# V as the stationary operand in two column groups, a joining product, split scores for two attentions, and the sink as a score column, in a fused four-layer attention kernel

## The chip, the cores and the metric

The kernel runs on one core of one Trainium2 chip. The metric is the device time of one execution in microseconds; a row of the profile is one core's.

## What is computed

Two blocks of two layers each follow one another on 512 rows of width 1024, with a context of 256 rows in the first block. Layer 1 has two attentions side by side, mla (8 heads, 96 wide, V 64 wide) and gqa (8 heads, 2 key heads, 64 wide), over 768 keys (512 rows and 256 of context). Layer 2 has win: 8 heads, 64 wide, a window of three blocks of 128 keys plus the context, and a sink logit per head that takes part in the softmax but has no V. Cut to its core:

```python
def joint_dense_attention(q, k, v, kc, vc):          # gqa and mla
    kk, vv = concat([kc, k]), concat([vc, v])
    sc = einsum('bqkgd,bnkd->bkgqn', qi, kk) * d ** -0.5
    p = softmax(sc)
    return einsum('bkgqn,bnkd->bqkgd', p, vv)

def joint_window_attention(q, k, v, kc, vc, sink):   # win
    s_loc = where(mask, einsum(qi, ki) * scale, NEG_INF)
    s_ctx = einsum(qi, kc) * scale
    p = softmax(concat([s_ctx, s_loc, s_snk]))
    return einsum(p[:l], vc) + einsum(p[l:l + 3 * Q_BLOCK], vi)
```

Layers 3 and 4 (attentions diff, fox and odd, V 128 wide) have the same structure and are not touched. All of it is float32.

## The kernel before

The work is written out by hand, engine by engine, with semaphores. `to(name, key)` increments one, `at(name, key)` waits for it. Each engine's program is strictly in the order written. TensorE's order sets that of everything else: projections in1 and up, attention gqa, attention mla, projections out1 and in2, attention win, out2, in3, attentions diff and fox, and so on.

Projections split both operands into a high and a low part in fp32r and add three products (L839 to L841). A plain fp32 matmul appears in the trace as two weight loads and two MATMUL instructions; one of split parts (fp32r) and a transpose (L1020, L954) as one each.

An attention is a list of units, one for a head and a tile t of 128 query rows. In gqa and mla a head has the units t = 0, 4, 1, 5, 2, 3: tiles 0 to 3 see all six blocks of 128 keys, tiles 4 and 5 (the context) two. In win a head has tiles 0 to 3 with 4, 5, 5 and 4 blocks. Iteration j of the loop works on three units at once:

- TensorE: the scores of unit j into banks 0 and 1 or 2 and 3 of PSUM (L994 and L995 for gqa, whose queries and keys are split into parts that are stacked to 128 rows; L997 for the others, in fp32); the transposes that prepare the next head's queries and keys (L954, into bank 7); the transposes of the probabilities of unit j-1 (L1020, first half of the blocks into bank 4, second into bank 5); the product with V of unit j-2 (L1032, into bank 6, with the turned probabilities as the stationary operand and 64 columns of V streaming). After that, beside the attention: every second iteration of gqa and every sixth of mla one 128-column piece of the modulation (L898, four column groups of 32, into bank 7), and in the iteration after it its turn (L907, bank 7).
- VectorE: the maximum of unit j (L1551, or L1553 with the mask added; scores are kept negated, so it is a minimum, `nmax`), in win also the sink's share in it (L1556); the copy of the first half of the turned probabilities of unit j-1 into `prT` (L1569); the scaling of unit j-2's result by 1/sum and the gate (L1580, L1597, called the mix; in win after adding `esink` to the sum, L1576).
- ScalarE: the copies of a preparation out of PSUM (L1206; for gqa L1200 and L1204, with VectorE's L1525 and L1529 for the low part); the exponentials of unit j (L1226), in win that of the sink (L1230); the copy of the second half of the turned probabilities of unit j-1 (L1240).

A preparation of 512 columns and one of 256 follow each other in the first iterations of the head before: in gqa two (queries), in mla four (keys, then queries). Every bank has a reader that the next writer waits for (`bank_free`): for bank 7 that is the last copy of a preparation, the copy of a modulation row (L1256) or VectorE's L1463. In the last iterations of mla and win the first transposes of the next projection (L809, bank 7) are put in as well. `ahead("out2")` on ScalarE, two weight splits (L1083), stands before win's attention.

## Time and profile before

| | us |
|---|---|
| runs (3) | 1721.02, 1722.75, 1725.63; median 1722.75 |
| the profiled execution | 1723.44 |
| its span | 1721.6 |
| TensorE busy | 1624.8 (94%) |
| TensorE weight loads | 1342.5 (78%) |
| VectorE busy | 899.1 (52%) |
| ScalarE busy | 647.5 (38%) |
| GpSimd busy | 566.9 (33%) |
| chain that ended last | TensorE 86%, VectorE 7%, ScalarE 3% |

The span runs from the first to the last instruction. Busy shares are means over stages with different limits, so the stages are read one by one below: gqa runs from 242 to 397 us, mla to 549, win from about 790 to 893. The mean granted TensorE clock is 0.971 of full speed. Weight loads overlap matmuls, so the two rows of TensorE don't add up.

### The profile page before, as it was taken

To read this page: it belongs to the slowest core of one execution; us is meant where nothing else is said; L and a number is where in the kernel's file an instruction comes from. 1 tells how busy PE (TensorE), PEld (TensorE's weight loads), DVE (VectorE), ACT (ScalarE), POOL (GpSimd) and SP (SyncE) were. 2 spreads that over 40 slices of the span, in tenths; PEclk is the share of its full clock that TensorE was granted. 3 is DMA by queue.
4 is the path that set the end of the run, shared out by engine and by line. 5 is a ranking of instruction groups with operands and counts; after the bars stand their busy time and mean duration, and the time that the engine had idled before them with its cause. 6 is when DMAs were issued, how large, how long until landed. Compare 5 with 4: busy or idle time off the path is not lost.

```text
span 1721.6 us, 24787 instructions
## 1 busy us (share of the span) xinstructions
PE 1624.8 (94%) x9120; PEld 1342.5 (78%) x9120; DVE 899.1 (52%) x2120; ACT 647.5 (38%) x1320; POOL 566.9 (33%) x333
## 2 busy tenths in 40 slices
PE   4999889899999979999999999989999999999998
PEld 1788878797887858887888789956578778887787
DVE  2655737665554244924752688036531279916422
ACT  3322354354454323334542433344333343336322
POOL 1222231860001333446505344410424534431134
PEclk9999989899999989999999999969999999999999
DMA  8321212231013112331003232300112222220222
GB/s 326 83 73 46 62 50 87 71 90 50 26 38 111 62 31 80 93 97 57 1 1 101 86 98 83 90 0 1 50 49 86 95 86 98 98 74 1 80 92 86
DMA packets 93158, 124.40 MB, mean 72 GB/s; under 512 B 10288, under 2 KB 52208, under 8 KB 92016
## 3 DMA queue, kind: packets, MB, share of 16 engines
q1 hardware_dynamic: 93040, 122.82, 22.5%
q8 instruction: 75, 1.23, 0.3%
q14 instruction: 43, 0.35, 0.1%
HBM read 120.70 MB, written 2.10 MB: 71 GB/s over the span
## 4 chain that ended last, share of the span: by engine, by line
PE 86%; DVE 7%; ACT 3%; issue 2%; DMA 1%; POOL 1%; SPq 0%; DVEq 0%; ACTq 0%; POOLq 0%
PE psum L839 18%; PE psum L841 18%; PE psum L840 18%; PE psum L1032 10%; PE psum L997 8%; PE psum L1020 5%; PE psum L809 3%; PE psum L954 3%; DMA mod_w<-mod_w_in 1%; PE psum L994 1%; PE psum L898 1%; PE psum L999 1%; PE psum L995 1%; ACT rz L1188 1%; DVE row_rstd L1346 0%
## 5 line engine op out<-in xcount | busy, mean ns | idle before, releaser
L1757 POOL TENSOR_TENSOR wlo<-wraw,whi 128x1024 fp32r<-128x1024 f32 (+4 forms) x172 | 399.7, 2325 | 979.1 <-ACT whi L1083 979.0
L1083 ACT ACTIVATE whi<-wraw 128x1024 fp32r<-128x1024 f32 (+4 forms) x172 | 174.7, 1019 | 483.3 <-PE psum L841 483.3
L839 PE MATMUL psum<-whi,h2h 128*128 128x512 f32 (+2 forms) x800 | 309.3, 387 | 7.1 <-ACT buf L1132 5.9
L841 PE MATMUL psum<-whi,h2l 128*128 128x512 f32 (+2 forms) x800 | 305.8, 382 | 0.0
L840 PE MATMUL psum<-wlo,h2h 128*128 128x512 f32 (+2 forms) x800 | 305.5, 382 | 0.0
L839 PE MATMUL psum<-whi,hTh 128*128 128x512 f32 (+2 forms) x512 | 196.9, 385 | 9.5 <-DVE hTl L1454 7.3
L1226 ACT ACTIVATE pr<-psum,nmax 128x512 f32<-128x512 f32 (+1 forms) x208 | 137.9, 663 | 170.9 <-DVE nmax L1551 88.3
L841 PE MATMUL psum<-whi,hTl 128*128 128x512 f32 (+2 forms) x512 | 192.0, 375 | 0.0
L840 PE MATMUL psum<-wlo,hTh 128*128 128x512 f32 (+2 forms) x512 | 192.0, 375 | 0.0
L839 PEld LDWEIGHTS psum<-whi,h2h 128*128 128x128 f32 x800 | 150.7, 188 | 33.4 <-issue 8.0
L997 PE MATMUL psum<-kT,qT 64*128 64x256 f32 (+5 forms) x480 | 164.6, 452 | 7.1 <-DVE qT L1536 4.3
L841 PEld LDWEIGHTS psum<-whi,h2l 128*128 128x128 f32 x800 | 150.6, 188 | 26.6
L840 PEld LDWEIGHTS psum<-wlo,h2h 128*128 128x128 f32 x800 | 150.7, 188 | 25.3
L1020 PE MATMUL psum<-ident,pr 128*128 128x128 f32 x792 | 130.6, 286 | 9.2 <-ACT pr L1226 7.2
L1020 PEld LDWEIGHTS psum<-ident,pr 128*128 128x128 f32 x792 | 94.8, 146 | 34.8 <-ACT pr L1226 18.6
L839 PEld LDWEIGHTS psum<-whi,hTh 128*128 128x128 f32 x512 | 98.0, 191 | 25.3 <-issue 9.7
L841 PEld LDWEIGHTS psum<-whi,hTl 128*128 128x128 f32 x512 | 97.9, 191 | 17.0
L840 PEld LDWEIGHTS psum<-wlo,hTh 128*128 128x128 f32 x512 | 98.2, 192 | 15.2
L1551 DVE TENSOR_REDUCE nmax<-psum 128x1 f32<-128x768 f32 x96 | 74.9, 780 | 65.9 <-PE psum L997 41.4
L997 PEld LDWEIGHTS psum<-kT,qT 64*128 64x128 f32 (+2 forms) x480 | 79.9, 193 | 35.7 <-issue 19.0
L1569 DVE COPY prT<-psum 128x256 f32<-128x256 f32 (+1 forms) x208 | 90.6, 435 | 23.3 <-PE psum L1020 21.1
L1032 PE MATMUL psum<-gq,prT 128*128 128x64 f32 x736 | 93.7, 274 | 1.1 <-DVE rz L1597 1.1
(253 smaller groups left out, 2459.8 us busy)
## 6 DMA issues: line engine op xcount, KB each, us to landing
wraw<-mod_w_in SPq DMA_DIRECT2D x32, 512.0 KB, 3.8
wraw<-w_in_odd_in SPq DMA_DIRECT2D x32, 512.0 KB, 3.4
wraw<-cd_w_in_in SPq DMA_DIRECT2D x24, 512.0 KB, 3.6
wraw<-w_in_even_in SPq DMA_DIRECT2D x20, 512.0 KB, 3.9
mod_w<-mod_w_in SPq DMA_DIRECT2D x8, 1024.0 KB, 17.8
wraw<-ab_w_in_in SPq DMA_DIRECT2D x16, 512.0 KB, 3.6
wraw<-w_ple_gate_in SPq DMA_DIRECT2D x16, 512.0 KB, 3.9
wraw<-ab_w_out_in SPq DMA_DIRECT2D x8, 512.0 KB, 3.6
```

Of the source, the lines that this page charges most:

```text
L809: mm = eng.transpose(psum[:, b, n_ * P:(n_ + 1) * P], turn[name]["rows"](t, k), ident[:, :])
L839: eng.matmul(dst, a[0], ww[0], start=first, stop=False)
L840: eng.matmul(dst, a[0], ww[1], start=False, stop=False)
L841: mm = eng.matmul(dst, a[1], ww[0], start=False, stop=last_)
L997: mm = eng.matmul(dst, q_, ks[0:dk, a:b], start=True, stop=name != "fox")
L1020: mm = eng.transpose(psum[:, bk, (b - b0) * P:(b - b0 + 1) * P], pr[:, i % 2, b * P:(b + 1) * P], ident[:, :])
L1032: mm = eng.matmul(psum[:, 6, 0:dv], prT[:, i % 2, n_ * P:(n_ + 1) * P], v_rows(name, h, b), start=n_ == 0, stop=n_ == len(bl) - 1)
L1083: eng.activation(whi[:, s, :, 0:w], wraw[:, u["id"] % RAW, :, 0:w], ACT.Copy).then_inc(*to("split_hi", u["id"]))
L1226: eng.activation(pr[:, j % 2, 0:w], psum_flat[:, s0 * 512:s0 * 512 + w], ACT.Exp, bias=nmax[:, j % 4:j % 4 + 1], scale=-1.0, accum_out=rsu ...
L1551: eng.tensor_reduce(m, sc, AX.X, ALU.min).then_inc(*(label or note("nmax", (name, j))))
L1569: eng.tensor_copy(prT[:, i % 2, 0:nb * P], psum[:, 4, 0:nb * P]).then_inc(*note("probs_a", (name, i)))
L1757: eng.tensor_tensor(wlo[:, s, :, 0:w], wraw[:, u["id"] % RAW, :, 0:w], f32(whi[:, s, :, 0:w]), ALU.subtract)\
```

## The change

The edits are these.

- The product with V in gqa, mla and win (`HALVED`): V becomes the stationary operand, 64 columns, and the turned probabilities stream, 128 columns. Blocks alternate between partitions 0 to 63 and 64 to 127 of bank 6, so that bank 6 holds two partial sums, transposed. ScalarE copies the 128x128 result to `o2`, and one more fp32 product (`joined`), with `o2` stationary and two stacked 64x64 identities (`halves`, loaded once by DMA) streaming, adds the two and turns them back into bank 6.
- The order in these three: TensorE issues scores, product with V, preparation and turns (second half first), what stands beside, and the join at the iteration's end. ScalarE: preparation, copy to `o2`, second half, exponentials. VectorE: maximum, low parts of a preparation, mix, first half.
- Scores: mla's queries and keys are split into high and low parts of fp32r (`PARTED`) and three products are added; win is stacked as gqa is (`STACKED`), two products over 128 rows. The low parts of mla lie in place of tensors that are free then.
- The sink of win: one more score column, by an fp32 product of the identity with a column of `nsink`. The exponentials and their sum take it in; the maximum starts from it. `esink` and the operations L1230, L1556 and L1576 go.

```diff
+    out["halves"] = np.concatenate([np.eye(64), np.eye(64)]).astype(np.float32)
...
-        STACKED = ("gqa",)
+        STACKED, PARTED = ("gqa", "win"), ("mla",)
+        ROUNDED = STACKED + PARTED
+        HALVED = ("gqa", "mla", "win")
...
+            key, _, _, tiles, dst, d = p_
+            if name in PARTED:
+                lo = (qTl if key[0] == "q" else kTl)[0:d, key[1] % 2, tiles[0] * P:(tiles[-1] + 1) * P]
+                return [dst], [lo]
...
+            load(halves[:, :], io["k_halves"], "load_sel", 1)
...
-                                if name in STACKED:
-                                    eng.wait_ge(*at("heads_copied", (name, p_[0], int(p_[0][0] == "k"))))
+                                if name in ROUNDED:
+                                    eng.wait_ge(*at("heads_copied", (name, p_[0], int(name in STACKED and p_[0][0] == "k"))))
...
+                            elif name in PARTED:
+                                eng.matmul(dst, q_, ks[0:dk, a:b], start=True, stop=False)
+                                eng.matmul(dst, q_, kTl[0:dk, h % 2, a:b], start=False, stop=False)
+                                mm = eng.matmul(dst, qTl[0:dk, h % 2, t * P:(t + 1) * P], ks[0:dk, a:b], start=False, stop=True)
...
+                        if name == "win":
+                            if j == 0:
+                                eng.wait_ge(*at("nsink", 0))
+                            c0 = s0 * 512 + cols_of(name, t)
+                            mm = eng.matmul(psum_flat[:, c0:c0 + 1], ident[:, :], nsink[:, h:h + 1], start=True, stop=True)
                         mm.then_inc(*to("scores", (name, j)))
+                    if name in HALVED and lag < j:
+                        i = j - lag - 1
+                        h, t = units[i]
+                        bl = blocks_of(name, t)
+                        nb0 = first_blocks(name, t)
+                        bank_free(6)
+                        for p_, n_ in enumerate([*range(nb0, len(bl)), *range(nb0)]):
+                            if p_ == 0 and nb0 < len(bl):
+                                eng.wait_ge(*at("probs_b", (name, i)))
+                            if n_ == 0:
+                                eng.wait_ge(*at("probs_a", (name, i)))
+                            c0 = 64 * (p_ % 2)
+                            mm = eng.matmul(psum[c0:c0 + 64, 6, 0:P], v_rows(name, h, bl[n_]), prT[:, i % 2, n_ * P:(n_ + 1) * P],
+                                            start=p_ < 2, stop=p_ >= len(bl) - 2)
+                        mm.then_inc(*to("product_v", (name, i)))
...
-                        for b0, b1, bk in ((0, nb0, 4), (nb0, nb, 5)):
+                        parts = ((0, nb0, 4), (nb0, nb, 5))
+                        for b0, b1, bk in reversed(parts) if name in HALVED else parts:
...
+                    if name in HALVED and lag < j:
+                        i = j - lag - 1
+                        eng.wait_ge(*at("o2_copied", (name, i)))
+                        eng.matmul(psum[:, 6, 0:dv], o2[:, i % 2, :], halves[:, :], start=True, stop=True)\
+                           .then_inc(*to("joined", (name, i)))
+                        reader[6] = ("mixed", (name, i))
...
-                    if name in STACKED:
+                    if name in ROUNDED:
                         highs = parts_of(name, p_)[0]
-                        eng.activation(highs[0], psum[0:64, prep_bank(name, p_), 0:len(tiles) * P], ACT.Copy)\
+                        eng.activation(highs[0], psum[0:DK[name], prep_bank(name, p_), 0:len(tiles) * P], ACT.Copy)\
                            .then_inc(*to("heads_copied", (name, key, 0)))
...
+                    if name in HALVED:
+                        if lag < j:
+                            i = j - lag - 1
+                            eng.wait_ge(*at("product_v", (name, i)))
+                            eng.activation(o2[:, i % 2, :], psum[:, 6, 0:P], ACT.Copy).then_inc(*to("o2_copied", (name, i)))
+                        if lag <= j < len(units) + lag:
+                            second_half(j - lag)
+                        if j < len(units):
+                            exp(j)
+                    else:
+                        if j < len(units):
+                            exp(j)
+                        if lag <= j < len(units) + lag:
+                            second_half(j - lag)
...
-                        if name == "win":
-                            eng.activation(esink[:, j % 4:j % 4 + 1], sink[:, h:h + 1], ACT.Exp,
-                                           bias=nmax[:, j % 4:j % 4 + 1]).then_inc(*to("exp_sink", j))
...
-                    eng.tensor_tensor(lows[0], psum[0:64, prep_bank(name, p_), 0:len(p_[3]) * P], f32(highs[0]), ALU.subtract)\
+                    eng.tensor_tensor(lows[0], psum[0:DK[name], prep_bank(name, p_), 0:len(p_[3]) * P], f32(highs[0]), ALU.subtract)\
...
+                    eng.wait_ge(*at("joined" if name in HALVED else "product_v", (name, i)))
...
-                        label = small() if name == "win" else None
                         if bias is None:
-                            eng.tensor_reduce(m, sc, AX.X, ALU.min).then_inc(*(label or note("nmax", (name, j))))
+                            eng.tensor_reduce(m, sc, AX.X, ALU.min).then_inc(*note("nmax", (name, j)))
                         else:
-                            eng.tensor_tensor_reduce(sc, sc, bias, 1.0, 3.0e38, ALU.add, ALU.min, m).then_inc(*(label or note("nmax", (name, j))))
-                        if name == "win":
-                            after_last()
-                            eng.tensor_tensor(m, m, nsink[:, h:h + 1], ALU.min).then_inc(*note("nmax", (name, j)))
+                            most = nsink[:, h:h + 1] if name == "win" else 3.0e38
+                            eng.tensor_tensor_reduce(sc, sc, bias, 1.0, most, ALU.add, ALU.min, m).then_inc(*note("nmax", (name, j)))
...
+                    if name in HALVED:
+                        if lag < j:
+                            mix(j - lag - 1)
+                        if lag <= j < len(units) + lag:
+                            first_half(j - lag)
+                    else:
+                        if lag <= j < len(units) + lag:
+                            first_half(j - lag)
+                        if lag < j:
+                            mix(j - lag - 1)
```

## Rows read from the trace of the kernel before

**Rows 1.** gqa and mla: busy of PE, PEld, DVE, ACT, POOL; clock

```profile
242.00:397.00 155.00, 142.26 (x1301) 127.32 (x1302) 107.76 (x268) 68.20 (x171) 76.77 (x83) 0.91 0.29 83
397.00:549.00 152.00, 148.40 (x1128) 123.67 (x1128) 80.62 (x208) 72.75 (x174) 1.67 (x1) 1.00 0.15 50
```

**Rows 2.** the chain that ended last in gqa, mla, win: start, us, what

```profile
350.11 1.29 PE psum L1032 x12
...
366.52 0.50 PE psum L1032 x5
...
482.54 1.29 PE psum L1032 x12
...
488.43 1.35 PE psum L997 x4
...
500.18 0.84 PE psum L1032 x8
...
854.30 1.06 PE psum L997 x4
...
857.41 1.28 PE psum L997 x6
...
865.75 0.41 PE psum L997
```

**Rows 3.** timeline, then line L881 (ns min/median/max, first and last start)

```profile
29.84 1.94 PE L881 MATMUL psum<-mod_w,silu_pad 128*32 128x512 f32 x8 [1.42 <-DMA mod_w<-mod_w_in]
...
L881 PE MATMUL psum<-mod_w,silu_pad x64: 592/1060/1062, 15.0 to 34.3; 128*32 128x512 f32 x64
```

**Rows 4.** timeline of TensorE around a modulation product in gqa

```profile
353.26 0.61 PE L1032 MATMUL psum<-gq,prT 128*128 128x64 f32 x4
353.80 0.64 PE L898 MATMUL psum<-wraw,silu_pad 128*32 128x128 f32 x16
354.38 0.39 PE L994 MATMUL psum<-kTs,qTs 128*128 128x256 f32 x1
354.60 0.28 PE L995 MATMUL psum<-kTs,qTs 128*128 128x256 f32 x1
```

**Rows 5.** timeline of TensorE around a unit's scores in win

```profile
806.58 1.23 PE L1032 MATMUL psum<-gq,prT 128*128 128x64 f32 x10
...
807.74 1.35 PE L997 MATMUL psum<-kT,qT 64*128 64x256 f32 x6
...
809.02 0.66 PE L1020 MATMUL psum<-ident,pr 128*128 128x128 f32 x4
```

**Rows 6.** the chain that ended last, split scores of gqa

```profile
351.57 0.34 PE psum L994
351.91 0.23 PE psum L995
352.13 0.12 PE psum L994
```

**Rows 7.** groups by form in mla (last: gqa): busy, mean ns | idle

```profile
L1569 DVE COPY prT<-psum 128x384 f32<-128x384 f32 x32 | 17.7, 553 | 2.7 <-PE psum L1020 1.7
...
L1597 DVE SCALAR_TENSOR_TENSOR rz<-psum,rinv,rz 128x64 f32<-128x64 f32 x48 | 13.6, 284 | 23.4 <-PE psum L1032 22.8
...
L1569 DVE COPY prT<-psum 128x256 f32<-128x256 f32 x16 | 6.6, 415 | 0.0
...
L1206 ACT ACTIVATE kT<-psum 96x512 f32<-96x512 f32 x7 | 4.2, 594 | 10.4 <-PE psum L954 10.4
...
L1256 ACT ACTIVATE mod_row<-psum 128x128 f32<-128x128 f32 x8 | 2.2, 278 | 4.3 <-PE psum L898 4.3
...
L1525 DVE TENSOR_TENSOR qTs<-psum,qTs 64x512 fp32r<-64x512 f32 x7 | 4.8, 684 | 2.4 <-ACT qTs L1200 2.3
```

**Rows 8.** timeline at win's start

```profile
790.79 1.99 ACT L1083 ACTIVATE whi<-wraw 128x1024 fp32r<-128x1024 f32 x2
...
792.56 1.10 PE L997 MATMUL psum<-kT,qT 64*128 64x256 f32 x4 [1.21 <-DVE qT L1536]
```

More of the change, by code:

```diff
@@ L187, in build @@
         fcum = sb("fcum", [P, NX, 4, 4])
+        ang, turns, mod_row = same_place([("ang", [P, NX, 24], F32), ("turns", [P, NX, 24], F32)], [("mod_row", [P, P], F32)])
         rx = sb("rx", [P, NT, D])
@@ L511, in temps @@
                 return qTs, kTs, pr1, prT1
-            return (qT1, kT1, pr1, prT1) if name in ("gqa", "mla", "win") else (qT2, kT2, pr2, prT2)
+            return (qTh, kTh, pr1, prT1) if name in PARTED else (qT2, kT2, pr2, prT2)
         def keys_of(name, g):
@@ L1529, in low @@
                         eng.tensor_copy(lows[1], f32(lows[0])).then_inc(*note("heads_lo", (name, p_[0])))
-                for p_ in preps[-1] if name in STACKED else ():
+                for p_ in preps[-1] if name in ROUNDED else ():
                     low(p_)
-                for p_ in preps[-1] if name not in STACKED else ():
+                for p_ in preps[-1] if name not in ROUNDED else ():
                     key, _, _, tiles, dst, d = p_
@@ L1536, in attention, with first_half, mix @@
                     eng.tensor_copy(dst, psum[0:d, prep_bank(name, p_), 0:len(tiles) * P]).then_inc(*note("heads_copied_v", (name, key)))
+                def first_half(i):
+                    nb = first_blocks(name, units[i][1])
+                    eng.wait_ge(*at("probs_turned", (name, i, 0)))
+                    if i >= 2:
+                        eng.wait_ge(*at("product_v", (name, i - 2)))
+                    eng.tensor_copy(prT[:, i % 2, 0:nb * P], psum[:, 4, 0:nb * P]).then_inc(*note("probs_a", (name, i)))
+                def mix(i):
+                    h, t = units[i]
+                    rs, ri = rsum[:, i % 4:i % 4 + 1], rinv[:, i % 4:i % 4 + 1]
+                    eng.wait_ge(*at("exps", (name, i)))
+                    eng.reciprocal(ri, rs).then_inc(*small())
+                    after_last()
+                    if name == "diff" and h % 2:
+                        eng.tensor_tensor(ri, ri, nlam[:, :], ALU.mult).then_inc(*small())
+                        after_last()
+                    eng.wait_ge(*at("joined" if name in HALVED else "product_v", (name, i)))
+                    o = psum[:, 6, 0:DV[name]]
+                    if name == "diff":
+                        dst = buf6[:, t, (h // 2) * P:(h // 2 + 1) * P]
+                        if h % 2 == 0:
+                            eng.tensor_scalar(dst, o, ri, None, ALU.mult).then_inc(*note("mixed", (name, i)))
+                        else:
+                            eng.scalar_tensor_tensor(out=dst, in0=o, scalar=ri, in1=dst, op0=ALU.mult, op1=ALU.add)\
+                               .then_inc(*note("mixed", (name, i)))
+                    else:
+                        c0 = {"gqa": 512 + h * 64, "mla": h * 64, "win": h * 64, "fox": 512 + h * P, "odd": h * P}[name]
+                        dst = rz[:, t, c0:c0 + DV[name]]
+                        eng.scalar_tensor_tensor(out=dst, in0=o, scalar=ri, in1=dst, op0=ALU.mult, op1=ALU.mult)\
+                           .then_inc(*note("mixed", (name, i)))
                 for j in range(len(units) + lag + 1):
```

106 lines of the change are left out of this document (34 added, 72 removed).

## The prediction

> **What bounds the kernel now.** I read the busy time by stage first. In the first of the three attentions concerned (gqa, 242 to 397 us) TensorE is busy 142 of 155 us, in the second (mla, to 549) 148 of 152 [rows 1]. Then the chain that ended last. In mla it is TensorE alone: a head goes from 482.54 to 500.18, 17.6 us; in gqa one takes 16.4 (350.11 to 366.52), in win 11.4 (854.30 to 865.75) [rows 2]. So TensorE's own work sets the pace of gqa and mla, and there a gain must come out of it, while any wait put into TensorE's order costs its full length. I call a unit of 6 blocks full and one of 2 blocks short; a head of gqa or mla is full, short, full, short, full, full.
>
> **The product with V.** Today 12 instructions (two per fp32 matmul) take 1.29 us [rows 2], 0.107 each, so a short unit's 4 take 0.43. Afterwards V is the weights, 64 columns wide, and 128 columns stream. Two questions: do the column groups overlap, and what does changing to them cost? The modulation shows both. At the start 8 instructions of 1.06 us each, in four groups of 32 columns, end within 1.94 us [rows 3], so groups do overlap. In gqa 16 such instructions, four rounds, come between full-width ones [rows 4]: the last full-width one begins at 353.60 (the fourth from 353.26, 0.11 apart; it ends at 353.87, so one lasts 0.27), the first narrow one at 353.80; the last narrow one at about 354.17, the next full-width one at 354.38 and its follower only at 354.60. Three gaps of 0.20 to 0.22 stand where 0.11 is usual: changing over and back costs about 0.32. The four rounds begin within 0.37, 0.109 a round after the first. The same gaps stand around win's scores, which use 64 rows of the array: the product's last begins at 807.54 (it ends at 807.81), the scores at 807.74, and the next instruction at 809.02, 1.28 later, where mla's rate (1,536 columns in 1.35) gives 1.12 for these 1,280 [rows 2, 5]. So a width of 64 changes mode like one of 32, and I charge 0.32 to each product: 6 rounds + 0.32 = 0.97 for a full unit (saves 0.32), 2 rounds 0.54 for a short one (costs 0.11), in win 0.76 for 4 blocks and 0.97 for 5 (save 0.10 and 0.09). The bounds: no change-over cost, 0.65 for a full unit; no overlap, 12 rounds and the change, 1.63.
>
> On the Trainium skill: its page "TensorEngine Tiling (Array Packing)", section "Stationary-Streaming Swap + Column Tiling", recommends just this swap for a right-hand side of up to 64 columns and puts it at up to 2x. By that rule alone a full product would be 0.65. The same page, section "Key Properties", says that a change of tiling mode drains the engine, which the gaps in rows 4 agree with, and that speaks against the change here, where every product is one short visit to the mode.
>
> **The join.** One fp32 product, 128 weight columns: two instructions, 0.21, on TensorE for every unit, 128 in all. Per head of gqa or mla: 4 x -0.32 + 2 x 0.11 + 6 x 0.21 = +0.2. Before it ScalarE copies 128x128 out of PSUM, 0.28 as L1256 takes for as much [rows 7].
>
> **Scores.** In mla the fp32 products of a full unit take 1.35 [rows 2]. Split parts stream 512 columns in 0.23 and 256 in 0.12, the first 0.11 more [rows 6]: 3 x 0.35 + 0.1 = 1.15, -0.2; a short unit stays at about 0.46. With the product, mla's head is -0.8 + 0.2 = -0.6. Win: 1.06 becomes 4 x 0.12 + 0.1 = 0.58, and 1.28 becomes 0.80 (its last two are bound by their weights, 0.11 each); -0.48 each. The sink column is one more fp32 matmul, 0.21 a unit. Win's head: 4 x (-0.48 + 0.21 + 0.21) - 0.4 = -0.6 of TensorE work. VectorE loses two operations on one column, ScalarE one; hardly any of it stands in win's chain.
>
> TensorE's work alone thus changes by 8 x (0.2 - 0.6 - 0.6) = -8 us.
>
> **The order, where I see the cost.** VectorE now mixes unit i before it copies the first half of unit i+1's turned probabilities, and the mix waits for the join. So from the join's end to a first half in place: 0.2 to reach VectorE, L1597 0.28, copy 0.55 (0.42 for 256), 0.04 back: 1.1 (0.95 for a short unit) [rows 7]. TensorE meanwhile has the next scores and, if there is one, the second half of the product (0.34 with the change-over). ScalarE takes a head's preparation (0.59 for 512 columns) ahead of the copy that the join needs, though TensorE issues the product ahead of the preparation's transposes; and in mla VectorE's subtraction (0.68) is new, also ahead of its mix [rows 7]. Through one head:
> - First iteration, both stages: the modulation's product stands in bank 7, where the preparation was. It now follows turns of 0.65 only (the 1.29 of the product went ahead of them), and the bank is free 0.3 + 0.59 + 0.04 + 0.68 = 1.6 after the transposes: wait 0.9.
> - Second: short scores (0.34 gqa, 0.46 mla) + 0.34 against 1.1: wait 0.4 and 0.3. Its modulation turn again waits for bank 7 (256 columns, about two thirds of that chain, 1.1, against 0.65 of turns): 0.4.
> - Third, mla only: the preparation's copy, then the join's, against short turns of 0.22: wait 0.9.
> - Fourth: a short unit's product against its copy: 0.95 less the scores, 0.6 and 0.5; mla's join another 0.25.
> - Fifth and sixth: 0.2.
>
> Sum: gqa 2.5, mla 3.5 a head, on top of +0.2 and -0.6 of work. Some of it overlaps, because one wait gives the next link time; following the queues through a whole head, with each engine's work in program order, I get a period of 18.6 us for gqa and 19.9 for mla, against 16.4 and 17.6, so +2.2 and +2.3. The last head prepares nothing: +1 and +0.5. Singly: gqa's second key group, whose four ScalarE copies (about 2.0) now stand ahead of a join, +1.5; mla's start, where split copies replace VectorE's, and its four late turns of the mix, +2. gqa 7 x 2.2 + 1 + 1.5 = +18; mla 7 x 2.3 + 0.5 + 2 = +18.5.
>
> Win has no short units and no modulation; its queues give a head of 10.7 against 11.4, 8 x -0.7 = -6. Against it: today VectorE copies keys and queries at once, and the scores begin at 792.56; in the changed order ScalarE must first finish two weight splits, at 792.78 [rows 8], then make five copies (2.6) and VectorE one subtraction: scores near 796.1, +3.5, of which TensorE stands idle nearly 5 us. Key group, late turns and the tail +2. Win: -0.5. Everything outside these three stages stays.
>
> Sum +18 + 18.5 - 0.5 = +36, against the profiled execution's own 1723.4 us (span 1721.6 and 1.8 around it), which is 0.7 above the median of the runs, 1722.75. I take 1 off for change-overs hidden under a wait: 1722.75 + 35, **1758 us**. Its own range, for waits half or one and a third as long: 1738 to 1772.
>
> **Rivals.**
> - *The waits are hidden and TensorE's work alone counts*: -8, 1715 us, faster. For it: rows 1 show VectorE and ScalarE busy half of mla, so capacity is there; it takes the first-half copy being ready within short scores + 0.34, i.e. the way from join to copy being under 0.8 rather than 1.1, and the bank-7 waits vanishing. Against: L1597 and L1569 alone are 0.84 [rows 7]. It decides below a mean wait of 0.2 us a unit in gqa and mla. Chance 0.2.
> - *64-column groups cost no change-over* (the skill's page above, at its up to 2x): -0.32 on each of 128 products; but the same queues then bind: gqa's head comes to 17.3, mla's to 18.9, win's to 9.8. +6, +9, -8: +7, 1730 us. For it: no row shows a group of 64 columns. Against: rows 5, where 64 rows behave as 32 columns do. Chance 0.15.
> - *No overlap of two groups*: full products 1.63, 4 blocks 1.20, 5 blocks 1.41, short 0.76: 64 x 0.66 + 16 x 0.44 x 2 + 32 x 0.22 = +63 more, 1821 us. Rows 3 speak against. Chance 0.03.
> - Something else (a lower clock after win's idle start, rows that I misread): 0.07.
>
> Forecast 0.55. The range that leaves out 2 in 10: 1717 to 1776. A measurement of this kernel can tell about 0.3%, 5 us, from no change. Faster 0.22 (the first rival and the low edge of the second), same 0.06, slower 0.72.
>
> **What the changed profile would show.** The product: rounds of 0.11 in two groups, gaps of 0.20 on both sides; if the instruction after it follows in 0.11, the second rival holds. TensorE waiting for VectorE's prT (L1569's successor) in products of short units, for qTs/kTl at the modulation, for the o2 copy at the join; these lines are hardly there today. TensorE's busy share of mla falls from 98% to about 88%, the head's period to 19 to 20 us. Win's heads shorter, its first scores 3 to 4 us later. If the periods are 16.5 and 17 with no such waits, my reading of the queues was wrong; if they are above 21, the product doesn't overlap.

## The result, and the profile after

The changed kernel takes 1771.9 us (median of 4 runs, 1769.5 to 1774.4), the kernel before 1722.7 on the same chip: a ratio of 1.028, 95% interval 1.026 to 1.031. That is 49 us slower; the forecast was 35 us slower, with a range to 1776. The span grows by 51.0 us, from 1721.6 to 1772.6. Measured between the first and last reductions of the scores' maxima (the line that writes nmax) in each stage, gqa takes 18.6 us more, the way from gqa to mla 1.8, mla 24.6, the way from mla's last to win's first 10.5, win 5.1 less, and everything else 0.5 more. In new line numbers the product is L1032, the turns of the probabilities L1055, the join L1081, the modulation's product L908 and its turn L917, the operands' turns L964, the copy of the half sums (o2, which the trace calls o) L1287, the copies of turned probabilities L1598 (VectorE) and L1273 (ScalarE), the low parts L1580 and L1584.

Windows over gqa and mla in the changed kernel, columns as in [rows 1]:

```profile
242.00:415.00 173.00, 147.77 (x1394) 114.59 (x1394) 110.98 (x265) 78.55 (x218) 76.49 (x83) 0.90 0.26 74
415.00:595.00 180.00, 153.41 (x1307) 120.99 (x1306) 96.13 (x240) 82.26 (x228) 0.22 (x1) 0.98 0.13 42
```

TensorE is busy 5 us more in each stage than in [rows 1], and the stages are 18 and 28 us longer: TensorE idles 25 us in gqa where it idled 13, and 27 in mla where it idled 4. Its busy share of mla is 85%.

The chain that ended last, in gqa and in win:

```profile
396.50 0.81 PE psum L1032 x12
397.31 0.81 PE psum L1055 x6
...
404.79 0.06 DVE rz L1622
...
404.99 0.42 DVE prT L1598
...
405.55 0.44 PE psum L1032 x4
...
910.33 0.27 ACT o L1287
...
910.64 0.43 PE psum L1081 x2
```

A full product is 0.81 where [rows 2] have 1.29, but the turns behind it are 0.81 where six took 0.65: the way back out of the narrow mode is booked there. The two together are the forecast's 0.97. In the kernel before the chain through this gqa head is TensorE alone. Here VectorE's mix and its copy of the turned probabilities stand in the chain, and ScalarE's copy ahead of the join.

The timeline of the same visit (engine, line, operation, tiles, count), and around a modulation product in mla:

```profile
396.23 0.28 PE L1005 MATMUL psum<-kTs,qTs 128*128 128x256 f32 x1
396.43 0.88 PE L1032 MATMUL psum<-prT,gq 128*64 128x128 f32 x12
397.25 0.87 PE L1055 MATMUL psum<-ident,pr 128*128 128x128 f32 x6
...
530.34 0.82 PE L1055 MATMUL psum<-ident,pr 128*128 128x128 f32 x6
530.54 0.59 ACT L1241 ACTIVATE kTh<-psum 96x512 fp32r<-96x512 f32 x1 [1.71 <-PE psum L964]
...
531.17 0.69 DVE L1580 TENSOR_TENSOR kTl<-psum,kTh 96x512 fp32r<-96x512 f32 x1 [1.05 <-ACT kTh L1241]
...
532.00 0.64 PE L908 MATMUL psum<-wraw,silu_pad 128*32 128x128 f32 x16 [0.84 <-DVE kTl L1580]
...
533.12 0.28 DVE L1622 SCALAR_TENSOR_TENSOR rz<-psum,rinv,rz 128x64 f32<-128x64 f32 x1 [1.19 <-PE psum L1081]
...
533.32 0.55 DVE L1598 COPY prT<-psum 128x384 f32<-128x384 f32 x1
```

The product starts 0.20 after the last full-width instruction instead of 0.11, and the turns 0.20 after its last. The modulation waits 0.84 us for the low parts to leave bank 7 (forecast 0.9), and the copy stands behind the mix (0.28), as read.

What TensorE waited for: the first two rows in gqa (250 to 415 us), the others in mla (415 to 595); sum, times, longest:

```profile
PE psum L908 <- DVE qTs L1580: 5.0, 6, 0.8
PE psum L1032 <- DVE prT L1598: 4.9, 8, 0.9
...
PE psum L908 <- DVE kTl L1580: 6.5, 7, 1.5
PE psum L1081 <- ACT o L1287: 6.2, 12, 0.6
PE psum L1032 <- DVE prT L1598: 4.4, 8, 0.7
```

L917 adds 2.4 us in gqa and 2.2 in mla. These are the waits that the forecast named. Win's start, which answers to [rows 8]:

```profile
840.08 1.25 PE L964 MATMUL psum<-ident,gq 128*64 128x128 f32 x10
...
840.78 1.99 ACT L1124 ACTIVATE whi<-wraw 128x1024 fp32r<-128x1024 f32 x2
841.90 4.83 POOL L1816 TENSOR_TENSOR wlo<-wraw,whi 128x1024 fp32r<-128x1024 f32 x2 [8.90 <-ACT whi L1124]
...
845.01 1.87 DVE L1584 CAST kTs<-kTs 64x256 fp32r<-64x256 f32 x1
...
846.80 0.68 DVE L1580 TENSOR_TENSOR qTs<-psum,qTs 64x512 fp32r<-64x512 f32 x1
...
847.95 0.55 PE L1004 MATMUL psum<-kTs,qTs 128*128 128x256 f32 x1 [6.61 <-DVE qTs L1580]
```

TensorE idles 6.6 us where nearly 5 was forecast. The copy of 256 columns of low parts from SBUF to SBUF takes 1.87: a GpSimd operation (the second of L1816) had begun before it and ended at 846.73, and the copy ended at 846.88. At the second key group of gqa in the kernel before, where no GpSimd operation was under way when it began, the same copy takes 0.29. The copy of 512 columns met the same thing in gqa: at the second key group of the changed kernel it began at 322.65, while a GpSimd operation ran that ended at 323.69, and took 1.32, where it takes 0.42 in the kernel before.

Two more things stand in this profile that the forecast hadn't. At mla's end ScalarE's first splits of the next projection's weights now come behind the last copy of the half sums:

```profile
593.48 0.28 ACT L1287 ACTIVATE o<-psum 128x128 f32<-128x128 f32 x1 [1.57 <-PE psum L1032]
593.65 1.99 ACT L1124 ACTIVATE whi<-wraw 128x1024 fp32r<-128x1024 f32 x2
...
597.18 0.80 PE L849 MATMUL psum<-whi,hTh 128*128 128x512 f32 x1 [2.93 <-POOL wlo L1816]
```

TensorE idles 2.93 us there, where the kernel before idles 0.60. And the granted clock stands at its lower level (1.2 GHz) for 136.9 us of the execution against 103.3, by the trace's clock records. The new stretches begin in such idle times or just behind them: at 347.5 (gqa, behind a wait of 1.7 us before a modulation product), 422.6 (mla's start), 596.7 (the wait above), 845.8 (win's start), 893.6 (win's second key group). 33.6 us at half speed cost at most 16.8.

### The profile page after: what moved, and what is told of

Same layout as the page of the kernel before. It is cut to its first block, busy times and chain, and to the rows that moved or that the text cites. A ratio compares the mean times of both kernels' runs of the same rounds, so it can differ in the third digit from the quotient of the medians.

```text
span 1772.6 us, 25698 instructions
## 1 busy us (share of the span) xinstructions
PE 1628.4 (92%) x9520; PEld 1324.8 (75%) x9520; DVE 907.5 (51%) x2097; ACT 673.5 (38%) x1427; POOL 566.0 (32%) x333
## 4 chain that ended last, share of the span: by engine, by line
PE 82%; DVE 9%; ACT 4%; issue 2%; DMA 1%; POOL 1%; SPq 0%; DVEq 0%; ACTq 0%; POOLq 0%
PE psum L849 17%; PE psum L851 17%; PE psum L850 17%; PE psum L1032 5%; PE psum L1055 4%; PE psum L1011 3%; PE psum L964 3%; PE psum L1067 3%; PE psum L819 3%; PE psum L1081 2%; DMA mod_w<-mod_w_in 1%; PE psum L1004 1%; PE psum L908 1%; PE psum L1005 1%; PE psum L1007 1%
## 5 line engine op out<-in xcount | busy, mean ns | idle before, releaser
L1816 POOL TENSOR_TENSOR wlo<-wraw,whi 128x1024 fp32r<-128x1024 f32 (+4 forms) x172 | 398.7, 2319 | 1024.1 <-ACT whi L1124 1024.0
L1261 ACT ACTIVATE pr<-psum,nmax 128x768 f32<-128x768 f32 (+2 forms) x208 | 138.1, 664 | 58.1 <-DVE nmax L1641 47.5
L1055 PE MATMUL psum<-ident,pr 128*128 128x128 f32 x792 | 133.8, 292 | 4.9 <-ACT pr L1261 3.6
L1055 PEld LDWEIGHTS psum<-ident,pr 128*128 128x128 f32 x792 | 93.5, 147 | 35.0 <-issue 20.6
L1622 DVE SCALAR_TENSOR_TENSOR rz<-psum,rinv,rz 128x64 f32<-128x64 f32 (+1 forms) x176 | 53.1, 302 | 102.6 <-PE psum L1081 89.0
L1598 DVE COPY prT<-psum 128x256 f32<-128x256 f32 (+1 forms) x208 | 90.0, 432 | 19.6 <-PE psum L1055 18.7
L1032 PE MATMUL psum<-prT,gq 128*64 128x128 f32 x736 | 65.8, 297 | 8.6 <-DVE prT L1598 4.9
L1011 PE MATMUL psum<-kT,qT 128*128 128x128 f32 (+7 forms) x160 | 66.0, 496 | 4.7 <-DVE qT L1591 2.0
```

The source lines that it names most:

```text
L1011: mm = eng.matmul(dst, q_, ks[0:dk, a:b], start=True, stop=name != "fox")
L1032: mm = eng.matmul(psum[c0:c0 + 64, 6, 0:P], v_rows(name, h, bl[n_]), prT[:, i % 2, n_ * P:(n_ + 1) * P], start=p_ < 2, stop=p_ >= len(bl) - 2)
L1055: mm = eng.transpose(psum[:, bk, (b - b0) * P:(b - b0 + 1) * P], pr[:, i % 2, b * P:(b + 1) * P], ident[:, :])
L1261: eng.activation(pr[:, j % 2, 0:w], psum_flat[:, s0 * 512:s0 * 512 + w], ACT.Exp, bias=nmax[:, j % 4:j % 4 + 1], scale=-1.0, accum_out=rsu ...
L1598: eng.tensor_copy(prT[:, i % 2, 0:nb * P], psum[:, 4, 0:nb * P]).then_inc(*note("probs_a", (name, i)))
L1816: eng.tensor_tensor(wlo[:, s, :, 0:w], wraw[:, u["id"] % RAW, :, 0:w], f32(whi[:, s, :, 0:w]), ALU.subtract)\
```

## The experiments

"Before" is in each case the kernel before on the same chip, 1721.6 to 1723.0 us. Head periods are between the nmax reductions of like units, for the last full head.

**The two parts apart.** The scores' part alone:

```diff
-        HALVED = ("gqa", "mla", "win")
+        HALVED = ()
```

> The product with V goes back to the form and the place that it had before, in all three attentions; mla keeps its split scores, win its stacked scores and the sink column. Theory (the halves' waits and change-overs are the loss, the scores are a gain): gqa's head goes back to 16.4 us; mla's is 17.6 less 4 x 0.2 to 1.3 for the scores, some 16.6; win's is 11.4 less 8 scores' gains, 9.5 to 10. Against that stand some 1.5 us at mla's start and 5.5 at win's start (the seven low parts of the key heads that the scores now wait for). Sum -8 + -14 + 7: 1705 to 1714 us. Rival (the low parts queued on VectorE are what costs mla its 3 us a head): mla's head stays at 19 or more, and the whole at 1722 or above.

Measured: 1732.5 us (ratio 1.006, 1.005 to 1.008). The heads came as the theory said: mla 16.61 (17.64 before), win's 9.99 to 10.76 (11.45 to 12.98) outside its start, its second key group and the stretch described next; the 10.76 has 1.5 us of that stretch in it. Mla took 3.8 us less from first to last nmax. Win took 7.7 us more, all in its second half. Windows there:

```profile
830.00:840.00 10.00, 7.70 (x70) 7.43 (x70) 8.29 (x21) 5.69 (x13) 9.47 (x8) 0.96 0.01 3
840.00:850.00 10.00, 9.35 (x45) 9.21 (x46) 4.36 (x12) 3.48 (x9) 1.64 (x2) 0.50 0.00 0
850.00:860.00 10.00, 10.00 (x50) 10.00 (x50) 4.07 (x13) 3.00 (x8) 0.00 (x0) 0.50 0.01 2
```

The granted clock (the column behind POOL) is 0.50 from 839.1 for 44.4 us though TensorE is full: it does 50 instructions in 10 us where it did 92 at full clock (810 to 830 us). Two heads took 17.87 us each. The fall comes in the idle time of the second key group (TensorE idles from 837.7); timeline:

```profile
839.05 1.26 POOL L1886 TENSOR_TENSOR cq<-cq,rz 128x512 f32<-128x512 f32 x1
839.11 1.48 DVE L1584 CAST kTs<-kTs 64x512 fp32r<-64x512 f32 x1
...
840.65 0.64 PE L964 MATMUL psum<-ident,gq 128*64 128x128 f32 x2 [2.95 <-DVE kTs L1584]
```

VectorE's copy of 512 columns, which begins 0.06 after a GpSimd operation, takes 1.48 where gqa's took 0.42, and TensorE idles 2.95. My theory of the heads held, and my total was wrong: the time lies 18 us above the top of what I expected.

The product's part alone (mla and win multiply their scores in fp32 as before, the sink stays a column):

```diff
-        STACKED, PARTED = ("gqa", "win"), ("mla",)
+        STACKED, PARTED = ("gqa",), ()
```

(two more lines make the operands of mla and win plain fp32 again)

> The product with V in two column groups with its join and its order, as in the changed kernel, but mla's and win's scores in the form of before (win's with the sink as a column). If the two parts only add, it comes at before + 49 + what the scores alone gained: 1775 to 1790 us. gqa as changed (18.9 a head), mla 17.6 + 2 to 2.8 = 19.6 to 20.4 a head (no low parts ahead of the copies on VectorE), win 11.4 + 0.5 to 1.2 = 12 to 12.6. Rival (the low parts delay the copies that the product needs, so that the two parts together cost more than each): mla's head falls to 18.5 and the whole lies under 1765.

Measured: 1776.3 us (1.032, 1.030 to 1.034), heads of 18.92, 20.00 and 13.07 us. The time, gqa and mla lie where they were expected; win's head is longer than the 12 to 12.6 that I gave it. So the whole loss comes with the product and its order. The parts don't quite add in mla: alone they change the head by +2.36 and -1.03, together by +2.77 instead of +1.33, so 1.4 us a head come from both at once. VectorE's low parts queue ahead of the mix and hold bank 7: without them the modulation's product waits 0.8 us for bank 7 in all of mla, with them 6.5.

**Do the groups overlap, and what does the mode cost?**

```diff
-                            c0 = 64 * (p_ % 2)
+                            c0 = 0
```

(with start and stop on the first and last block, and o2 and halves cut to 64 partitions)

> All blocks of a product go to partitions 0 to 63, one after the other, so no two groups overlap; the copy and the join take 64 partitions. The rest is the changed kernel. Theory (two groups run at once, and the change-over is paid for any 64-column weights): a full product takes 6 x 0.213 + 0.32 = 1.6 us instead of 0.97, a short one 0.75 instead of 0.54, so 16 heads x 3 us and win's 32 units x 0.5: about 1830 us. Rival (the change-over belongs to two groups being in use, not to narrow weights): gaps around the product fall to those inside it, a full product is 1.28 us, and the whole 1795 to 1805 us.

Measured: 1841.6 us (1.070, 1.067 to 1.073), 12 more than the theory's figure and far from the rival's. Timeline of one visit:

```profile
410.93 0.28 PE L1005 MATMUL psum<-kTs,qTs 128*128 128x256 f32 x1
411.14 1.52 PE L1032 MATMUL psum<-prT,gq 128*64 128x128 f32 x12
412.60 0.87 PE L1055 MATMUL psum<-ident,pr 128*128 128x128 f32 x6
```

Start to start 1.46 here, 0.82 in the changed kernel; so two groups do overlap, and that is worth 70 us. The gaps on both sides are 0.21 and 0.20 as in the changed kernel, with a single group in use: the change-over doesn't come from using two groups. The third rival and the second fall together.

It isn't paid for every instruction with 64 columns of weights, though, as I had it. The turns of gqa's and win's operands have such weights too (128*64), in the kernel before as well:

```profile
315.13 0.41 PE L954 MATMUL psum<-ident,gq 128*64 128x128 f32 x2 [1.85 <-DVE kTs L1529]
315.37 0.82 PE L1020 MATMUL psum<-ident,pr 128*128 128x128 f32 x6
```

The full-width turns begin 0.24 after the first of two, so no gap of 0.20 stands between them. At full clock the step from the last such turn to a full-width one is 0.11 in all 19 places in the three stages of the kernel before and all 15 in those of the changed one; the step from a product in halves to such a turn is 0.20. The 64-column turns behave like full-width instructions; the 64-column products don't. No run here shows why.

**The order.** First VectorE's copy ahead of its mix:

```diff
+                        if lag <= j < len(units) + lag:
+                            first_half(j - lag)
                         if lag < j:
                             mix(j - lag - 1)
-                        if lag <= j < len(units) + lag:
-                            first_half(j - lag)
```

> VectorE copies the first half of the turned probabilities before it mixes the unit before it, in place of after; nothing else moves. Theory (this order makes TensorE wait for the copy in the short units, 4.9 us of waits in gqa and 4.4 in mla, and as much again in win's start of heads): those waits go, and 6 to 10 us with them: 1762 to 1766 us. Rival (mixing later holds bank 6, and the next product waits instead; or the waits move on to the join): within 3 us of the changed kernel, 1769 to 1775.

Measured: 1759.5 us (1.022, 1.020 to 1.024), 12.5 less than the changed kernel and a little more than the 6 to 10 expected. The waits for L1598 went and some of them came back as waits for the mix; waits in mla:

```profile
PE psum L1081 <- ACT o L1287: 5.2, 10, 0.6
PE psum L1032 <- DVE rz L1622: 3.2, 8, 0.4
```

gqa's head fell by 0.85, mla's by only 0.3. Of gqa's 15.4 us some 7 are the heads; two stretches at the lower clock (they begin at 333.8 and 347.5 in the changed kernel, 17 us together, worth at most 8.5) went too.

Then, on top, ScalarE's o2 copy ahead of the operands' copies:

```diff
+                    if name in HALVED and lag < j:
+                        i = j - lag - 1
+                        eng.wait_ge(*at("product_v", (name, i)))
+                        eng.activation(o2[:, i % 2, :], psum[:, 6, 0:P], ACT.Copy).then_inc(*to("o2_copied", (name, i)))
                     for p_ in preps.get(j, []):
                         prep(p_)
...
                     if name in HALVED:
-                        if lag < j:
-                            i = j - lag - 1
-                            eng.wait_ge(*at("product_v", (name, i)))
-                            eng.activation(o2[:, i % 2, :], psum[:, 6, 0:P], ACT.Copy).then_inc(*to("o2_copied", (name, i)))
```

> As the run with the copy of the first half ahead of the mix (1759.5 us), and on ScalarE the copy of the two halves' sums (o2) also goes ahead of the copies of the next head's turned operands. Theory (the join waits behind those copies, 5.2 us of waits in mla in that run): about 3 to 5 us less, 1754 to 1757 us. Rival (the operand copy that is passed is itself waited for, by the modulation product through bank 7): those waits grow by as much, and the time stays at 1757 to 1762 us.

Measured: 1756.6 us (1.020, 1.018 to 1.021), 2.9 less, at the edge of what can be told. Its waits in mla:

```profile
PE psum L1032 <- DVE rz L1622: 9.9, 9, 1.3
```

The join's waits are gone and the product waits for the mix instead, 9.9 us where it was 3.2. Neither of my theories had that: the wait moved one link on. The time lies in the range of my theory all the same, but mla gave only 1.2 us of it, so that is luck.

Next, instead, TensorE's turns of the next head's operands ahead of the product (with the copy first on VectorE):

```diff
+                    for p_ in preps.get(j, []):
+                        prep(p_)
                     if name in HALVED and lag < j:
...
                         mm.then_inc(*to("product_v", (name, i)))
-                    for p_ in preps.get(j, []):
-                        prep(p_)
```

> As the run with the copy of the first half ahead of the mix (1759.5 us), and on TensorE the turns of the next head's operands go ahead of the product with V instead of behind it; ScalarE's order is unchanged and then fits. Theory (the modulation product, its turn and the join wait for bank 7 and for the o2 copy because too little TensorE work lies between the operands' turns and them): the waits on L908, 6.5 us in gqa and as much in mla, and most of those on the join go: 8 to 14 us less, 1746 to 1752 us. Rival (the product then waits for bank 6 or for its probabilities all the same, so that the waits only move): 1757 us or more.

Measured: 1731.6 us (1.005, 1.004 to 1.007), 28 less than without the move and twice what I expected. Heads 16.79 (gqa), 17.29 (mla), 9.77 (win). Window over mla, then the same place in a head as above:

```profile
403.00:545.00 142.00, 138.29 (x1223) 110.01 (x1222) 92.65 (x223) 80.49 (x213) 0.00 (x0) 0.98 0.16 53
...
494.43 0.59 ACT L1241 ACTIVATE kTh<-psum 96x512 fp32r<-96x512 f32 x1 [0.78 <-PE psum L964]
495.05 0.69 DVE L1580 TENSOR_TENSOR kTl<-psum,kTh 96x512 fp32r<-96x512 f32 x1
...
495.93 0.65 PE L908 MATMUL psum<-wraw,silu_pad 128*32 128x128 f32 x16
```

With 0.81 of product between, the low parts leave bank 7 at 495.74, before the modulation needs it, and TensorE is busy 97% of mla again. Its waits in mla, where the run without the move had 6.5 and 5.2:

```profile
PE psum L908 <- DVE kTl L1580: 1.5, 1, 1.5
PE psum L1081 <- ACT o L1287: 1.0, 3, 0.4
```

One move heals the bank, the modulation's turn (2.2 us of waits before, none now) and the join, because each had been late by the same preparation.

What keeps this form behind the kernel before stands mostly outside the heads: gqa measures +1.2 us, mla +3.0, win -7.6, and the way from mla's last reduction to win's first +10.4, which holds the wait at mla's tail and win's start.

The move alone, with VectorE's order left as changed:

> The changed kernel with one move: on TensorE the turns of the next head's operands go ahead of the product with V. VectorE mixes before it copies, as in the changed kernel. Theory (the operands' turns and the copy's order are two separate causes, since the operands are turned beside the first units of a head and the copy is late in its last, short units): the 28 us that the move gave on top of the other order are given here too, 1742 to 1748 us. Rival (the move gives the copy its time as well, so the order on VectorE no longer matters): 1735 us or less.

Measured: 1742.2 us (1.012, 1.009 to 1.014), as the theory said: two separate causes, the operands' place worth 28 to 30 us and the copy's place 11 to 12.5.

**What is left of the product.** I summed, for the last full head of mla, the times from each TensorE instruction's start to the next one's start (a wait or a change-over is booked on the instruction ahead of it), in us; where the head is cut shifts a term by 0.1 or so:

```
                     scores  product  turns  join  operands  modulation  sum
before                 6.43     6.03   3.17     -      1.24        0.78  17.65
scores only            5.59     5.92   3.06     -      1.24        0.77  16.58
changed                6.67     4.21   5.80  1.47      1.48        0.80  20.43
operands first         5.78     3.97   3.83  1.37      1.62        0.71  17.28
```

With the waits nearly gone, the product in halves gives 1.95 us a head against the scores alone and takes back 1.37 for the join, 0.77 at the turns, 0.19 at the scores and 0.38 at the operands: 0.7 us worse than the product it replaces. In this mla head the way of doing it doesn't pay, nor in gqa, whose head is 16.79 where it was 16.43.

**The slow copy.** With the scores alone, the second low part is taken from PSUM again:

```diff
-   eng.tensor_copy(lows[1], f32(lows[0]))
+   eng.tensor_tensor(lows[1], psum[0:DK[name], prep_bank(name, p_), 0:len(p_[3]) * P], f32(highs[0]), ALU.subtract)
```

> As the run with the scores alone (1732.5 us), with one instruction changed on VectorE: the second copy of a key's low parts is the subtraction from PSUM once more, not a copy from SBUF to SBUF, which took 1.5 to 1.9 us beside GpSimd's work where it took 0.54 without. Theory (that copy waits for GpSimd, and the wait at win's second key group is what the clock falls after, 44 us at half clock from there): win starts 1.5 us sooner, the key group waits under 2 us instead of 3.0, the half clock shrinks to 7 us or none, and the whole comes at 1708 to 1718 us. Rival (the half clock belongs to the idle time before win's start and to what follows it, whatever this copy does): 1727 to 1731 us, 1.5 to 3 us from the copies alone.

Measured: 1714.0 us (0.995, 0.9935 to 0.9965), 18.5 below the same kernel with the copy. Win's second key group, and windows around it:

```profile
835.35 0.68 DVE L1584 TENSOR_TENSOR kTs<-psum,kTs 64x512 fp32r<-64x512 f32 x1
...
836.09 0.62 PE L964 MATMUL psum<-ident,gq 128*64 128x128 f32 x2 [2.15 <-DVE kTs L1584]
...
830.00:840.00 10.00, 7.85 (x55) 7.55 (x55) 6.43 (x20) 5.59 (x13) 8.59 (x7) 0.81 0.01 2
840.00:850.00 10.00, 10.00 (x79) 9.71 (x78) 6.47 (x20) 4.47 (x11) 0.00 (x0) 0.85 0.00 0
```

0.68 beside GpSimd instead of 1.48, a wait of 2.15 instead of 2.95, and 6.8 us at the lower clock instead of 44.4. Win measures 16.4 us less. That the slow copy is what made the stretch long isn't shown: the clock fell at 839.1, as that copy began, and the last experiment has executions as long as 1730 to 1738 us without it. (The 0.54 that I had called the copy's time without GpSimd is one that had met it too; without it the copy takes 0.42.)

The same with TensorE kept at work in that wait:

```diff
                         prep(p_)
+                        if name == "win" and p_[0][0] == "k":
+                            keep_clock(16)
```

> As the run before it, and TensorE does 16 idle turns of the identity (1.75 us) behind each of the two key turns of win's second key group, in the wait that stands there. Theory (the half clock in win follows from TensorE's idle time at the key group): no half clock in win from 840 us on, or one of 7 us at most; win's eight heads at 10 us each but for the key group: 1706 to 1714 us. Rival (not the idle time there, but what came before it): the half clock stays 44 us long and the whole at 1727 us or above.

Measured: 1713.2 us (0.995, 0.993 to 0.997). The profile shows no stretch at the lower clock in win after its start, where the run without it has 6.8 us behind the key group. The time is that of the run without it: what was gained there stays within the scatter (1708.5 to 1719.2).

The same edit of the copy in the changed kernel with the operands first:

> As the run with the operands' turns ahead of the product and the copy ahead of the mix (1731.6 us), and with the second low part of a key subtracted from PSUM instead of copied from SBUF. Theory (that copy stands in the wait at each second key group and at win's start): 1 us at win's start, 1.5 us at each key group, 3 us of half clock in gqa: 1724 to 1728 us, which is no better than before since the product in halves itself gains nothing. Rival (with the clock kept up in gqa and win as well the changed form passes the kernel before): under 1719 us.

Measured: 1727.6 us (1.0036, 1.0022 to 1.0049). As forecast: the repaired form of the change doesn't reach the kernel before.

And in the kernel before:

> The kernel before with the same single edit (the second low part of gqa's keys subtracted from PSUM). It says how much of the 8 us by which the scores alone with this edit lie below the kernel before is the edit's own. Theory (in gqa's second key group it shortens the wait and the half clock, as it did with the scores alone, where gqa went from 147.9 to 144.4 us): 1717 to 1720 us, so that mla's and win's split scores are worth some 5 us. Rival (the edit is the whole gain): 1714 us or less.

Measured: 1717.7 us (0.9975, 0.9964 to 0.9985). The time is as expected and the reason isn't: gqa went from 147.8 to 144.3 us, but the copy got longer (0.68 for 0.42; it hadn't met a GpSimd operation under way there) and the wait in the key group too (2.1 for 1.9). What fell is the stretch at the lower clock behind it, 3.4 us for 10.2. Half of those 6.8 us are the 3.4 by which gqa fell, so its gain is a matter of the clock. What turned the clock isn't shown.

**Win's start.** ScalarE's copies of win's first operands ahead of the two splits:

```diff
                 for p_ in preps[-1] if name in ROUNDED else ():
                     prep(p_)
+                if between is not None:
+                    ahead(between)
...
-            ahead("out2")
-            attention("win")
+            attention("win", between="out2")
```

> The scores alone with the second low part subtracted from PSUM (1714.0 us), and on ScalarE the three copies of win's first operands go ahead of the two splits of the next projection's weights (1.99 us) instead of behind them. Theory (those splits, then the chain of copies and subtractions, are what TensorE idles 5.3 us for at win's start): the first scores come 1.8 to 2.0 us after the projection's last product sooner, 3.3 to 3.5 us idle instead of 5.3, and with less idle time a shorter half clock there: 1709 to 1713 us. Rival (ScalarE isn't what comes last; VectorE's subtractions are): the wait stays above 4.5 us and the time at 1713 to 1716 us.

Timeline:

```profile
787.01 0.42 DVE L1585 TENSOR_TENSOR kTs<-psum,kTs 64x256 fp32r<-64x256 f32 x1
787.12 1.99 ACT L1124 ACTIVATE whi<-wraw 128x1024 fp32r<-128x1024 f32 x2
...
788.50 0.55 PE L1004 MATMUL psum<-kTs,qTs 128*128 128x256 f32 x1 [3.42 <-DVE qTs L1581]
```

The idle time is 3.42 us, as the theory had it. The time isn't as forecast, and it isn't settled: 12 runs lie between 1707.9 and 1737.9, their median is 1725.0 (ratio 1.000, 0.998 to 1.002, over the ten shortest), and they follow the mean granted clock, 0.966 in the shortest, 0.955 in those near 1725, 0.949 in the longest. The profile is of an execution of 1713.1. The time of 1714.0 with the splits ahead had a clock of 0.960 to 0.965 in its 4 runs, on another chip; so few runs may not show all that that kernel does. Why the clock falls for long in some executions and not in others is open; no profile of a long one of this kernel was taken.

## Why the prediction was right, and where it was 14 us short

The time lies at the top of the forecast's own range (1738 to 1772). The mechanism is the one forecast: waits at the named places outweigh what TensorE's work gains. Part of the agreement in the single stages is luck, as said below.

- *TensorE's own work, -8 us for the three stages.* The terms held singly: full product 0.97 with its change-over (measured 0.81 and 0.16 at the turns behind it), short 0.44 and the same 0.16, so 0.60 (forecast 0.54), win's scores 0.53 (0.58), the sink 0.11 to 0.17 (0.21), the join 0.23 (0.21). Mla's head fell by 1.03 with the split scores alone, of which the scores themselves are 0.84 (forecast 0.8). With the operands first and the waits mostly out, the last full heads come at 16.79, 17.29 and 9.77 us: +0.4, -0.35 and -1.7 against before. Eight of each would make -13 us, where the work alone was put at -8, but first and last heads and key groups come out worse: the three stages measure +1.2, +3.0 and -7.6, -3.4 together. No run shows the work without any wait. Mla's and win's gain is the scores': the scores alone give -1.03 in mla and -0.7 to -1.8 in win's last full heads.
- *The waits.* Each named wait is in the trace, at its place: bank 7 (0.84 for 0.9), the copy behind the mix, the join behind ScalarE's operand copy, the short units' products. That they are what costs is shown by taking them out: 40 us of the 49 went with two moves in the order and no change of the work. The clock can be at most 5 of these 40: the stretches at its lower level are 126.5 us there and 136.9 in the changed kernel. The size was a little low: +2.5 and +2.8 us a head for +2.2 and +2.3. The step that fell short is the period "by following the queues" in mla, 19.9 for 20.4; the sum of its single waits before that correction, 3.5, is nearer.
- *gqa, +18:* measured 18.6, and the total agrees better than its parts. Head by head from the first it is +1.1, +2.0, +2.9, +6.4, +0.7, +2.6, +2.5 and +0.4, where 2.2 each and 1 for the last was forecast with 1.5 for the second key group. The +6.4 lies there: VectorE's copy of low parts took 1.32 beside GpSimd there, not 0.42. *mla, +18.5:* measured 24.6 from first to last nmax, and 1.8 between the stages. Its three last full heads are 2.75 longer, the three with late turns or the spread of the modulation 3.1, the first 4.3 (partly at the lower clock), the last six units 2.8; the forecast was 2.3 each, 0.5 for the last, and 2 for start and late turns.
- *Win, -0.5 in all.* Heads and key group -5.1, forecast -4. The start was +5.4 from the operands' turns to the first scores, not +3.5: VectorE's copy beside GpSimd, 1.87 for 0.29, accounts for 1.6 of the 1.9 between them.
- *"Everything outside these three stages stays"* was a step that failed. Mla's tail on ScalarE has one copy more before the next projection's splits: +2.3 us of idle time, in all runs with the product in halves and in none without.
- *The clock* was in the forecast only as a part of "something else". At most 17 us of the 51 are its doing; the new stretches stand in or behind new idle times. How much of it exactly isn't shown, since a stretch costs only what TensorE would have done in it.
- *The rivals.* "The waits are hidden" fell: they aren't. "No change-over" and "no overlap" fell with the run on one group and with the gaps of 0.20. The trace of the kernel before did hold instructions with 64 columns of weights, the operands' turns, and they have no such gaps. Had I read them, they would have spoken for "no change-over", and wrongly: the win scores on 64 rows, on which the forecast rested, were the better guide.

The Trainium skill's "TensorEngine Tiling (Array Packing)", section "Key Properties", says that a change of mode drains the engine. The gaps of 0.20 around the products agree. The visits here have 4 to 12 instructions and pay the same gaps; what a longer one would give wasn't tried.

## What to carry to other kernels

A new form of a piece of work that saves 2 us a head on the busy engine can cost three through its order. Write down each new link (here product, copy, join, mix, copy), and for each what its engine must do first. Then look for one early item that makes several links late: here it was the turns of the next head's operands, which lacked the 0.81 us of product behind them. Try such a move before judging the change. And read the granted clock of each stage beside every total: here, with the scores alone, a wait of 2.95 us went with 44 us at half speed, and the same heads with 2.15 us of waiting with 7.

## What the runs showed of the hardware

- Products with weights 64 columns wide have gaps around them even if only one group is used: 0.20 to 0.21 instead of 0.11 on the way in and out, and about 0.05 more before the second instruction each time, 0.29 a visit. Turns with weights 64 columns wide have none (0.11 to the full-width instruction behind them). Two groups of such products run fully beside each other (0.82 for 1.46 us).
- A VectorE copy of fp32 from SBUF to SBUF that began early in a GpSimd tensor operation took 1.21 to 1.84 us for 512 columns and 1.25 to 1.87 for 256, and ended 0.15 to 0.28 behind the GpSimd operation; in gqa of the kernel before, where it began first, 0.42 and 0.29. The subtraction that reads PSUM took 0.68 and 0.42 with and without GpSimd beside it. The Trainium skill, "SBUF — State Buffer", section "SBUF: two separate sides", has the rule: a port pair that the two share goes, for the whole instruction, to whichever starts first of a GpSimd operation and a VectorE operation of certain kinds (one in a 2-port performance mode, which an fp32 copy from SBUF to SBUF triggers, or one with two inputs in SBUF). The traces agree with it in these cases.
- The length of a stretch at the lower clock doesn't follow the wait ahead of it alone: at win's second key group it is 44.4 us with a wait of 2.95 (one profile; the four runs of that kernel, 1730 to 1735 us, all have a mean clock of 0.951 or 0.952), 6.8 with one of 2.71 in the changed kernel and 6.8 with one of 2.15 with the direct subtraction. In the last experiment the mean clock goes from 0.949 to 0.966 from one execution to the next of one kernel.
